# Which queue asks for the experts' down weights: SyncE's or ScalarE's

## The reference

```python
def moe_swiglu(x, w_router, w_gate, w_up, w_down):
    logits = (x @ w_router).astype(jnp.float32)
    top_vals, top_idx = lax.top_k(logits, TOP_K)
    weights = jax.nn.softmax(top_vals, axis=-1)
    combine = jnp.sum(jax.nn.one_hot(top_idx, N_EXPERTS) * weights[..., None], axis=-2)
    out = jnp.zeros_like(x)
    for e in range(N_EXPERTS):
        out = out + combine[..., e:e + 1] * swiglu(x, w_gate[e], w_up[e], w_down[e])
    return out
```

## Time and profile before

| | |
|---|---|
| median of 3 runs | 1523.0 us (1522.2 to 1523.5) |
| profiled execution, its own time | 1521.5 us |
| its span, first to last instruction | 1519.7 us |
| TensorE busy in the span | 1476.3 us (97%) |
| mean granted TensorE clock | 0.989 |
| expert stage, from TensorE's first expert matmul to its last | 601.3 to 1474.4 us |
| moved by DMA over the span | 468.46 MB, mean 308 GB/s |

### The profile page before, as it was taken

How to read it: one execution, slowest core, us unless ns; L and a number is a source line. 1 busy time by engine, 2 the same in 40 slices (tenths; PEclk the granted TensorE clock), 3 DMA queues, 4 the chain that set the end, 5 groups by cost and what they waited for, 6 DMA issues and landing times.

```text
span 1519.7 us, 33431 instructions
## 1 busy us (share of the span) xinstructions
PE 1476.3 (97%) x14993; PEld 1029.4 (68%) x14993; DVE 701.8 (46%) x1581; ACT 327.4 (22%) x466; POOL 42.0 (3%) x50
## 2 busy tenths in 40 slices
PE   7999899999899998999999999999999999999987
PEld 6888788888678877767666555555555555556665
DVE  5785665555774677323233232323233232323356
ACT  4543344443345554000000000000000000000022
POOL 2010100000100000000000000000000000000020
PEclk9999999999999999999999999999999999999998
DMA  9866445555345335999999999999999999999960
GB/s 372 308 230 213 145 166 196 210 173 193 136 150 197 112 100 223 391 390 411 410 410 406 409 411 402 411 410 406 411 406 410 402 411 405 411 406 409 404 236 28
DMA packets 196094, 468.46 MB, mean 308 GB/s; under 512 B 7741, under 2 KB 8433, under 8 KB 195441
## 3 DMA queue, kind: packets, MB, share of 16 engines
q1 hardware_dynamic: 191392, 450.92, 77.8%
q0 software_dynamic: 2992, 12.70, 2.2%
q10 hardware_dynamic: 1568, 2.75, 0.5%
HBM read 462.53 MB, written 3.81 MB: 307 GB/s over the span
## 4 chain that ended last, share of the span: by engine, by line
PE 92%; DVE 5%; ACT 1%; DMA 1%; issue 1%; DVEq 0%; ACTq 0%
PE ps L1543 90%; PE ps L1560 1%; DVE acc L1001 1%; DVE stats L1010 0%; DMA ws_raw<-in_gm_w_s_dram 0%; DVE htl L973 0%; ACT split L613 0%; PE ps L1763 0%; DVE h L1006 0%; DVE split L958 0%; PE ps L1860 0%; PE ps L1896 0%; ACT hth L628 0%; DVE m_bt L1485 0%; ACT prob L803 0%
## 5 line engine op out<-in xcount | busy, mean ns | idle before, releaser
L1543 PE MATMUL ps<-ring,xt 128*32 128x256 f32 (+1 forms) x8064 | 625.9, 451 | 1.1 <-DVE m_hb L1477 1.1
L1543 PEld LDWEIGHTS ps<-ring,xt 128*32 128x32 f32 x8064 | 360.7, 109 | 226.3 <-DVE m_hb L1477 1.6
L1543 PE MATMUL ps<-split,hth 128*128 128x512 f32 x1184 | 374.3, 398 | 8.7 <-DVE htl L973 4.5
L1543 PE MATMUL ps<-ring,m_bt 128*32 128x256 f32 (+1 forms) x4032 | 335.8, 451 | 0.6 <-DVE m_bt L1485 0.6
L1473 DVE TENSOR_TENSOR m_hb<-ps,m_sg 128x256 f32<-128x256 f32 x56 | 23.8, 425 | 567.0 <-ACT m_sg L896 556.3
L1543 PEld LDWEIGHTS ps<-split,hth 128*128 128x128 f32 x1184 | 223.6, 191 | 56.0 <-DVE htl L973 7.8
L1543 PEld LDWEIGHTS ps<-ring,m_bt 128*32 128x32 f32 x4032 | 183.4, 109 | 112.7 <-DVE m_bt L1485 1.0
L1485 DVE STREAM_TRANSPOSE m_bt<-m_hb 32x96 f32<-32x96 f32 x896 | 241.4, 269 | 13.1
L1543 PE MATMUL ps<-split,htl 128*128 128x512 f32 x592 | 233.5, 394 | 0.0
L896 ACT ACTIVATE m_sg<-ps 128x256 f32<-128x256 f32 x56 | 21.6, 387 | 788.2 <-PE ps L1543 788.2
L958 DVE TENSOR_TENSOR split<-raw,split 128x2048 fp32r<-128x2048 f32 x50 | 114.0, 2291 | 77.7 <-ACT split L613 77.6
(11 more groups left out here) (234 smaller groups left out, 661.1 us busy)
## 6 DMA issues: line engine op xcount, KB each, us to landing
ring<-in_moe_w_gate_dram SPq DMA_DIRECT2D x112, 1024.0 KB, 11.7
ring<-in_moe_w_up_dram SPq DMA_DIRECT2D x112, 1024.0 KB, 12.7
ring<-in_moe_w_down_dram SPq DMA_DIRECT2D x112, 1024.0 KB, 11.7
raw<-in_gm_w_in_dram SPq DMA_DIRECT2D x14, 1024.0 KB, 13.3
raw<-in_ffn_w_gate_dram SPq DMA_DIRECT2D x14, 1024.0 KB, 5.0
raw<-in_ffn_w_up_dram SPq DMA_DIRECT2D x14, 1024.0 KB, 6.0
raw<-in_ffn_w_down_dram SPq DMA_DIRECT2D x14, 1024.0 KB, 4.9
raw<-in_fox_w_in_dram SPq DMA_DIRECT2D x12, 1024.0 KB, 5.0
```

Source lines behind the costliest of these rows:

```text
L1543: return nc.tensor.matmul(o, a, b, start=start, stop=stop)
```

## The change

For blocks 1 to 55 the two down loads are no longer issued by SyncE. ScalarE issues them in a new function `load_down(b + 1)`, directly behind the two silu instructions of block b, without a wait of its own: ScalarE has at that point already waited for gate_up(b), which frees both slots. SyncE leaves these positions out, their waits too, and goes on with gate and up loads in the same order. The down loads of block 0 stay on SyncE. In `store`, nothing changes, but its two DMAs now share ScalarE's queue with the down loads.

```diff
+    LATER_DOWN = [down_at(b) + k for b in range(1, NB) for k in range(2)]
...
                 for k in range(2):
-                    if n == down_at(b) + k:
+                    if b == 0 and n == down_at(b) + k:
                         sp.dma_start(flat(ring[:, slot]), rows(moe_w_down[0, e], j * W + k * 2 * P))\
                             .then_inc(landed, 16)
...
-            else:
+            elif n not in LATER_DOWN:
                 sp.wait_ge(streams[0]["used"], G_MOE + n - RING + 1)
             ring_load(n)
...
+        def load_down(b):
+
+            e, j = divmod(b, NJ)
+            for k in range(2):
+                n = down_at(b) + k
+                act.dma_start(flat(ring[:, RING_SLOT[n % RING]]), rows(moe_w_down[0, e], j * W + k * 2 * P))\
+                    .then_inc(ring_landed[n % RING], 16)
+
...
                 nc.scalar.activation(m_sg[:, 2 * P:NQ], ps[1][:, 0:P], ACT.Silu).then_inc(e_silu, 1)
+                if b < NB - 1:
+                    load_down(b + 1)
                 if j == 0 and e:
                     store(e - 1, used0 + (G_MOE + down_at(b - 1) + 2),
```

More of the change, by code:

```diff
@@ L474, in _ @@
                         sp.wait_ge(gx_full, (r + 1) * (2 * KD))
-                    sp.wait_ge(streams[0]["used"], G_MOE + r * N_RING + n - RING + 1)
+                    if n not in LATER_DOWN:
+                        sp.wait_ge(streams[0]["used"], G_MOE + r * N_RING + n - RING + 1)
                     ring_load(n)
```

## The result

The changed kernel takes 1526.4 us, against 1523.1 us for the kernel before (medians of 20 executions each). The ratio is 1.0024, with a 95% interval of 1.0018 to 1.0030: slower by 3.7 us (2.7 to 4.6). One of the changed kernel's executions took 5442.2 us; it is left out of the ratio, and nothing on record shows its cause. The forecast was 1527.9 us, in a range of 1521 to 1537.

A forecast was written before the change was run, and what follows sets the result against it. TensorE was taken as the bound, with the DMA almost full. Lag 3.8 plus overtaking 5.1 + 5.1 makes 14.0 us against a cover of 9.1, so 4.9 us of wait on 1523.0: 1527.9 us, range 1521 to 1537.

The forecast's parts named there:

- Nothing gained on SyncE, nothing lost on ScalarE: Expert stage: removing SyncE's 110 issues and waits is worth 0; two issues a block in ScalarE's idle time cost 0.
- Lag of the start: Start of expert stage: later down(1) leaves the DMA idle 5.1 us, less a 1.3 us gap: 3.8 us behind.
- Overtaking: Late blocks: down pairs on ScalarE's queue pass older gate and up loads, delaying them 5.1 us per pair, 10.2 in all.
- The bound of 0: Low end for overtaking in late blocks: 0 us if ScalarE's queue gets only what SyncE's queue leaves.
- the second pair: Block 55: down(55), issued at 1448.4, finds the up load still in flight and passes it too, another 5.1 us.
- Cover: Block 55: its last up load lands at 1448.8 and is used at 1457.9, leaving 9.1 us.
- The cover did not hold: Late blocks: the rival that the cover holds, TensorE never waits and time stays 1523.0 us; chance 0.31.
- a rate higher by 0.6%: Expert stage: DMA moving 0.6% more would remove 5 of the 14 us, so no wait; chance 0.31.
- A lower rate: Expert stage: two mixed streams cost DMA rate, 8.5 us for each 1%, giving 1536.4 us; chance 0.15.
- rival 1: Late blocks: same time, 1523.0 us, as the cover holds and TensorE never waits; chance 0.31.
- gain in the tail: Tail: TensorE may get another clock after waiting, a few us faster at most, about 1519 us; chance 0.06.
- ScalarE held: Expert stage: ScalarE's issues held 2.52 us or longer, silu late only from 15 us on; 1530 us, chance 0.03.

The follow-up runs named there:

- e1: The change, but block 1's two down loads stay on SyncE, so ScalarE issues only those of blocks 2 to 55; 1524.3 us, ratio 1.0017.
- e8: Kernel before, SyncE held at load position 14 until gate_up(1) ended, and ScalarE issuing the down loads of blocks 40 to 55; 1537.9 us, ratio 1.0105.
- e6: Kernel before, one queue, SyncE holding load position 14 and all behind it until gate_up(1) ended; 1531.0 us, ratio 1.0054.
- e2: Kernel before, one queue, SyncE holding load position 14 until gate_up(0) ended, giving the change's late start alone; 1523.5 us, ratio 1.0004.
- e9: The change with down(1) on SyncE and each later down pair issued only after the next gate_up's first half; 1524.3 us, ratio 1.0012.
- e5: The change, with SyncE also held at load position 16 until gate_up(1) ended, for more lag at the start; 1533.0 us, ratio 1.0071.
- e4: Kernel before, with ScalarE issuing only the down loads of blocks 40 to 55 and no late start; 1522.9 us, ratio 1.0010.
- e3: The change limited to blocks 1 to 28, SyncE issuing the down loads of 0 and 29 to 55; 1522.6 us, ratio 1.0002.

## Why the prediction was right, and which terms were off

The forecast was slower by 4.9 us through waits of TensorE in the last blocks, and that came out: 3.63 us in the stage, 3.7 us by the ratio. Term by term:

*Nothing gained on SyncE, nothing lost on ScalarE*: right. The period is 15.54 us in the other blocks, the issues on ScalarE take 0.46 us in the median and at most 1.1, and idle time ahead of silu is still 14.99 us.

*Lag of the start, 3.8 us*: right at 20 us, 3.8 by the bytes, but only 1.7 us from 100 us on. The step that failed is "as it is full from then on, it never makes this up". It was not full yet: between 20 and 100 us the DMA of the kernel before had more gaps than the one from 618 to 621 that I had subtracted, and the late one filled them (660 to 680 us: 388 GB/s before, 411 in the change). The earlier trace rows showed it: slices 17 and 18 are 391 and 390 GB/s, which I had counted among the full ones. Later it isn't made up: 0.92 MB behind at 700 us, 2.3 us.

*Overtaking, 5.1 + 5.1 us*: right in size. From e1, 1.76 + 8.0 = 9.8 us; from e8 against e6, 10.6, of which up to 3.0 are the clock. The bound of 0, where the second queue gets only what the first leaves, is excluded by e8. It is not the same everywhere. At block 41 the up load of the second half had 12.9 us of cover in e2, with one queue, and 7.9 in the change: 5.0 us, one pair. At block 54 it had 6.3 in e2, and in the change TensorE was 0.86 us late and waited 2.56 more: 9.7 us, two pairs. That the second pair is part of it is shown also by e9's profile, where issuing later takes most of it away. In the profile the wait comes in block 54 and not, as in my working, in block 55. The Trainium skill (DMA: Bandwidth & Descriptors, "Queues, rings and completion order") has the engines take turns between queues with work, a packet at a time. The trace agrees in the main: the down loads landed in 9.4 us in the median while up loads went to 20.9, and from 1424 to 1428 us, with both queues full, q10 had 299 packets and q1 250. In bytes that was 1.16 MB against 0.48, as q10's packets are twice as large, so the turns favoured the down loads.

*Cover, 9.1 us*: 8.0 by e6 with its lag at 100 us; with its lag at 700 us, 5.70 MB or 14.0 us, it would be 8.6. I had measured it at block 55 only and taken the blocks before to have about the same. They have more: read as landing against use of the second half's up load, the kernel before has 23.1 us at block 3, 14.0 at block 50, 10.9 at block 52 and 8.8 at block 55. The last step down comes behind the four gathers of table rows that GpSimd issues at 1384 to 1387 and at 1424 us, 2.10 MB or 5.1 us of DMA on their own queue, q0; that they cause it is not tested. The waits of the change, e1 and e6 all come from block 51 on. e5, with more lag, has its first at block 23.

With these, lag + 9.8 - 8.0: the change 3.5 (measured 3.63), e4 1.8 (2.13), e8 15.1 (16.02), e5 10.1 (11.07), e2 and e3 nothing (0, 0). Two numbers, taken from e6 and e1, give the others within 1 us. Part of that is luck: without the clock's share of their last waits, e8 would be 13.0 and e5 9.2, and e8 then misses by 2.1 us.

*The rivals.* The cover did not hold, by 3.6 us; a rate higher by 0.6% wasn't there. A lower rate wasn't either (under 0.1% against the kernel before). By the sentence of the Trainium skill that I cited for rival 1 (DMA: Bandwidth & Descriptors, "Issuing engines are not separate DMA queues") only SyncE's issue time would change; the bytes per second agree with it, the order in which loads land does not, and the order is what cost. No gain in the tail, no ScalarE held.

## What to carry to other kernels

Here, with the DMA engines full, a second queue added no bandwidth; it changed who was served first, in favour of the moved loads. Before moving loads to it, measure the cover of the loads that stay (landing against first use, block by block, as it can shrink by half along the stage), and subtract the DMA time of every moved load that can be in flight beside them. If that is negative, keep the order of use in one queue, or issue the moved loads late. In this kernel the compute set the pace while the transfers fell behind by about 1% of the time (9 us of cover from block 3 to block 50), which showed nowhere until the last blocks: landing times by stage show it, busy shares don't.

## What the runs showed of the hardware that I had not expected

A wait of TensorE can cost more than its length. In e8 it waited 3.38 us at 1227.66, and the 72 matmuls behind took 8.14 us in place of 5.39. Windows of e8 (PE, PEld, DVE, ACT and POOL busy, granted clock, DMA share, GB/s):

```profile
1220.00:1224.00 4.00, 4.00 (x54) 2.20 (x48) 0.00 (x0) 0.00 (x0) 0.00 (x0) 1.00 1.03 414
1224.00:1228.00 4.00, 0.62 (x6) 0.23 (x8) 0.00 (x0) 0.00 (x0) 0.00 (x0) 0.81 1.04 416
1228.00:1232.00 4.00, 4.00 (x32) 1.96 (x28) 0.00 (x0) 0.00 (x0) 0.00 (x0) 0.50 1.03 411
1232.00:1236.00 4.00, 4.00 (x53) 2.32 (x49) 0.00 (x0) 0.14 (x1) 0.00 (x0) 0.84 1.02 390
```

The granted clock went from 1.00 to 0.50, which is 1.2 GHz in place of 2.4, and the 3.38 us of wait became 6.36 us of delay. It need not turn out so: the change's wait of 2.56 us was followed by matmuls of the normal 5.39 us. Nor does the length of the wait decide it. In e5 a shorter wait was followed by slow matmuls, with a granted clock of 0.61 in the mean from 1182 to 1185 us:

```profile
1182.44 7.07 PE L1556 MATMUL ps<-ring,xt 128*32 128x512 f32 x72 [2.19 <-DMA ring<-in_moe_w_up_dram]
```

e6's wait of 2.30 us at 1394.91 was too. What else decides it stays open here. While TensorE was slow the DMA went on at 411 GB/s, so part of such a loss is cover for the blocks behind, unless no block behind has to wait.

In the change only the engine with the crowded queue was held: on SyncE an up load's issue on q1 took up to 8.6 us, in the same stage in which ScalarE's issues on q10 took 0.37 to 1.1 us.
